# More of the gates' products behind the first scores of the sliding attention, fewer between its later units

## The reference, cut to what matters

```python
proj = u @ w_in            # xr, gr, q, k, v, g_rnn, g_attn
y_rnn  = rglru_branch(xr, gr, ...)          # recurrence, times gelu(gr)
y_attn = swa_sink_branch(q, k, v, sinks, cos, sin)
merged = sigmoid(g_rnn) * (y_rnn @ w_br_rnn) + sigmoid(g_attn) * (y_attn @ w_br_attn)
return merged @ w_out
```

## Time and profile before

| | |
|---|---|
| median of three runs | 2773.03 us (2770.18 to 2775.43) |
| the profiled execution | 2768.93 us, its span 2767.1 us |
| TensorE busy | 2613.5 us, 94% of the span |
| VectorE, ScalarE, GpSimd busy | 1281.7, 1090.0, 834.0 us |
| mean granted TensorE clock | 0.971 of full speed |
| sliding attention, layer 0 | 842.40 to 957.01 us of the span |
| sliding attention, layer 1 | 1834.22 to 1950.73 us |

### The profile page before, as it was taken

How to read it: one execution, slowest core, us unless ns; L and a number is a source line. 1 busy time by engine, 2 the same in 40 slices (tenths; PEclk the granted TensorE clock), 3 DMA queues, 4 the chain that set the end, 5 groups by cost and what they waited for, 6 DMA issues and landing times.

```text
span 2767.1 us, 30648 instructions
## 1 busy us (share of the span) xinstructions
PE 2613.5 (94%) x12190; PEld 2084.0 (75%) x12190; DVE 1281.7 (46%) x1841; ACT 1090.0 (39%) x1696; POOL 834.0 (30%) x354
## 2 busy tenths in 40 slices
PE   7889999999988999998999999989999999999997
PEld 5567877777765688877878888756788878788886
DVE  1775636767557646644351011466358353610113
ACT  2235224656445637323232122337365233332222
POOL 3220010000031244433234344322344432344444
PEclk9888999999999999999999999999999999999999
DMA  5141236889721133333123333221233331224232
GB/s 189 49 130 46 81 120 232 322 336 354 257 73 46 48 98 98 94 103 109 54 84 93 113 99 99 70 60 47 81 95 99 110 104 62 76 92 122 91 92 76
DMA packets 220077, 318.56 MB, mean 115 GB/s; under 512 B 17184, under 2 KB 176032, under 8 KB 219808
## 3 DMA queue, kind: packets, MB, share of 16 engines
q1 hardware_dynamic: 201184, 284.00, 32.2%
q10 hardware_dynamic: 16592, 24.72, 2.6%
q0 software_dynamic: 2160, 7.89, 0.8%
HBM read 300.81 MB, written 15.75 MB: 114 GB/s over the span
## 4 chain that ended last, share of the span: by engine, by line
PE 85%; DVE 8%; PEld 2%; ACT 2%; issue 2%; DMA 1%; ACTq 0%; PEldq 0%; DVEq 0%; POOL 0%
PE ps L624 79%; PE ps L771 3%; PE ps L636 3%; PEld ps L624 2%; DVE stats L1994 1%; DVE rows L2004 1%; DVE pair_l L2262 1%; DMA rows<-in_x 1%; DVE x_lo L1922 1%; DVE xc L2123 0%; DVE shift L2023 0%; ACT w_hi L1383 0%; ACT pair_h L1599 0%; DVE rows L2016 0%; DVE qf L2353 0%
## 5 line engine op out<-in xcount | busy, mean ns | idle before, releaser
L588 POOL TENSOR_TENSOR w_lo<-w_raw,w_hi 128x1024 fp32r<-128x1024 f32 x331 | 811.9, 2464 | 1554.7 <-ACT w_hi L1383 1554.7
L624 PE MATMUL ps<-x_hi,w_hi 128*128 128x512 f32 (+1 forms) x1624 | 656.1, 404 | 24.5 <-DVE x_lo L1922 16.3
L624 PE MATMUL ps<-x_lo,w_hi 128*128 128x512 f32 (+1 forms) x1624 | 642.1, 395 | 0.0
L624 PE MATMUL ps<-x_hi,w_lo 128*128 128x512 f32 (+1 forms) x1624 | 638.4, 393 | 0.0
L1383 ACT ACTIVATE w_hi<-w_raw 128x1024 fp32r<-128x1024 f32 x331 | 340.3, 1052 | 451.2 <-PE ps L624 447.8
L624 PEld LDWEIGHTS ps<-x_hi,w_hi 128*128 128x128 f32 (+1 forms) x1624 | 308.3, 190 | 110.6 <-POOL w_lo L588 21.7
L624 PEld LDWEIGHTS ps<-x_lo,w_hi 128*128 128x128 f32 (+1 forms) x1624 | 307.8, 190 | 70.4
L624 PEld LDWEIGHTS ps<-x_hi,w_lo 128*128 128x128 f32 (+1 forms) x1624 | 308.5, 190 | 68.8 <-issue 2.7
L2497 DVE TENSOR_TENSOR fhd<-fsg,ps 128x512 f32<-128x512 f32 x44 | 30.2, 687 | 391.8 <-PE ps L624 391.7
L2262 DVE TENSOR_TENSOR pair_l<-pair_raw,pair_h 128x2048 fp32r<-128x2048 f32 x84 | 189.8, 2287 | 47.1 <-ACT pair_h L1599 47.0
L1599 ACT ACTIVATE pair_h<-pair_raw 128x2048 fp32r<-128x2048 f32 x84 | 157.7, 1909 | 3.0 <-ACT yb L1614 2.8
(11 more groups left out here) (404 smaller groups left out, 4299.9 us busy)
## 6 DMA issues: line engine op xcount, KB each, us to landing
w_raw<-in_w_in SPq DMA_DIRECT2D x100, 512.0 KB, 3.7
w_raw<-in_ffn_wi SPq DMA_DIRECT2D x88, 512.0 KB, 3.5
pair_raw<-in_w_gate SPq DMA_DIRECT2D x56, 512.0 KB, 5.7
pair_raw<-in_w_up SPq DMA_DIRECT2D x56, 512.0 KB, 7.0
pair_raw<-in_w_down SPq DMA_DIRECT2D x56, 512.0 KB, 6.5
w_raw<-in_ffn_wo SPq DMA_DIRECT2D x44, 512.0 KB, 3.6
w_raw<-in_w_out SPq DMA_DIRECT2D x24, 512.0 KB, 3.6
kv_raw<-in_ckv_w SPq DMA_DIRECT2D x20, 512.0 KB, 4.5
```

What stands on the lines that cost most here:

```text
L588: pool.tensor_tensor(w_lo[:, slot, :], w_raw[:, slot, :], w_hi[:, slot, :].bitcast(F32), ALU.subtract).then_inc(lo_done, 1)
L624: ins = pe.matmul(o, a, b, start=first, stop=last)
```

## The change

TensorE's steps of the gates' products are dealt out differently: 8 behind the scores of unit 0, 2 behind unit 1, 1 behind unit 2, then 2 in each unit u, but only 1 where u % 7 is 2 or 5. The sum stays 64. Between the units that is 53 steps instead of 62, so nine are moved ahead. ScalarE's copies of the products and its splits of the slabs get written positions in place of the two conditions. Both layers have it. No instruction is added, removed or changed in size.

```diff
+    FILL_FIRST = (8, 2, 1)
+
+    def fill_steps(u):
+        return 1 if u % 7 in (2, 5) else 2
+
+    GATE_AT = (3, 7, 11, 16, 20, 25, 30, 34)
+    SPLIT_AT = (3, 5, 12, 15, 22, 25, 31, 33)
...
                 beside = gates_beside()
-                window_scores(0)
-                next(beside)
-                window_scores(1)
-                next(beside)
-                window_scores(2)
+                for u, steps in enumerate(FILL_FIRST):
+                    window_scores(u)
+                    for _ in range(steps):
+                        next(beside)
...
                     if u < last:
-                        next(beside)
-                        next(beside)
+                        for _ in range(fill_steps(u)):
+                            next(beside)
...
-                    if x >= 5 and x % 4 == 1:
-
-                        n = (x - 5) // 4
+                    if x in GATE_AT:
+                        n = GATE_AT.index(x)
                         product(n)
                         act.activation(mg[:, n, :], ps[:, 2 + n % 2, :], ACT.Copy).then_inc(s["evacuated"], 1)
-                    if x % 8 == 7 or (x % 8 == 1 and x > 1):
+                    if x in SPLIT_AT:
                         split(1)
```

More of the change, by code:

```diff
@@ L357, in build @@
     UNITS3 = [(i, p) for i in range(NT) for p in range(X_HEADS // 2)]
+    FILL_FIRST = (8, 2, 1)
+    def fill_steps(u):
+        return 1 if u % 7 in (2, 5) else 2
+    assert sum(FILL_FIRST) + sum(fill_steps(u) for u in range(len(UNITS2) - 1)) == KD * KD
+    GATE_AT = (3, 7, 11, 16, 20, 25, 30, 34)
+    SPLIT_AT = (3, 5, 12, 15, 22, 25, 31, 33)
     def width1(unit):
```

## The result

The changed kernel takes 2753.25 us (median of five runs, 2751.06 to 2759.23), the one before 2770.18 (five runs, 2769.36 to 2775.43). The ratio is 0.9936, 95% interval 0.9921 to 0.9951: 0.64% faster, 16.9 us between the medians. The profiled executions took 2768.93 and 2751.06 us, with spans of 2767.1 and 2749.3 us, 17.8 us apart. The forecast was a gain of 15.1 us.

What follows compares the result with a forecast made beforehand. TensorE was taken as the bound, with 6.4 us idle per layer before unit 1's scores, then half clock. 2 x (0.8 + 5.8) + 1.9 = 15.1 us off 2773.0 gave 2757.9 us; own range 2754 to 2763, 8-in-10 range 2753 to 2767.

Steps and rivals of the forecast that it cites:

- Part A: More steps behind the first scores: TensorE idles 1.8 us instead of 6.4, unit 3's scores 0.8 us sooner per layer.
- R4: Rival: steps behind the first scores wait for the second slab; margin 1.2 us, no time of its own, no chance given.
- Part B: Nine steps fewer between the units: 6.2 us minus 0.4 for VectorE lateness and GpSimd meetings, 5.8 us per layer.
- Part C: Layer 1's longer slow clock after the first scores: its extra 1.9 us goes if the clock doesn't fall.
- Part D: ScalarE's written positions for copies and splits: worth 0, at worst 1.6 us per layer.
- the best sum: Upper bounds over both layers: 2 x (0.9 + 6.2) + 1.9 = 16.1 us gain.
- 15.9 us without stalls: Gain over both layers if nothing stalled, set against 38 us of possible loss from GpSimd's subtractions.
- R1: Rival: the clock still falls after the first scores' remaining idle time; 6.5 us lost, 2764.4 us; chance 0.12.
- the row with 0.69: Evidence for a falling clock: idle 1.5 us at 1383.8, then mean clock 0.69 over the next 3.7 us.
- R2: Rival: ScalarE's and VectorE's latency sets the units' pace; only 3.5 us won, 2769.5 us; chance 0.09.
- R3: Rival: GpSimd's 16 subtractions hold up VectorE and so TensorE; at worst 38 us lost, 2795 us; chance 0.07.

Runs made afterwards that it cites:

- subtractions apart: Kernel before, its two splits at the tenth query evacuation moved to x = 1 and 3 of the units' loop; stages 111.81 and 113.05 us, whole 2763.91 us.
- single steps early: Changed kernel with its nine one-step units side by side at units 0 to 8, copies and splits matched; stages 110.41 and 110.40 us, whole 2757.45 us.
- clock alone: Kernel before plus 21 throwaway matmuls behind unit 0's scores, no work moved; stages 113.83 and 113.81 us, whole 2769.22 us.
- single steps late: Changed kernel with eight one-step units at units 23 to 30, copies and splits matched; stages 107.61 and 107.58 us, whole 2755.13 us.
- ten steps first: Changed kernel with ten steps behind the first scores, one-step units 0 to 2 and 23 to 30; stages 107.34 us, whole 2753.47 us, ratio 0.9931.

## Why the prediction came out as it did

**What bounds it: right.** The hole before unit 1's scores, VectorE as its cause and GpSimd behind that were read from the earlier trace rows; the run with the subtractions apart shows 3.8 of the 6.4 us to be GpSimd's hold.

**Part A, 0.8 us per layer: right.** The scores of unit 3 come 11.87 us after those of unit 0 instead of 12.63, 0.76 us sooner, with 11 steps done. The idle time is 1.71 us where 1.8 was worked out. The second slab was there in time, so R4 fell.

**Part B, 5.8 us per layer: too small.** From the scores of unit 3 on, 101.98 us became 95.74 in layer 0, 6.24, which is the full 9 x 0.69 us. The 0.4 us that I took off for VectorE being late at unit 9 and for meetings with GpSimd did not occur in either layer, though the meetings did: a division held for 2.54 us cost TensorE nothing. This is the term of the sum that was mis-sized: 5.8 where 6.24 was measured, 0.8 us over both layers. The single steps early show that the fear had its place (2.8 us), but not with the steps spread as they are.

**Part C, 1.9 us: right.** The layers are equal now; the run with the clock alone gives 2.70 - 0.78 = 1.92 us for it. The 1.9 us were taken from the one profile of before that the result is also measured against; whether another execution has the same difference is not shown.

**Part D, nothing: right as a sum, and too light as a warning.** All eight split places fit: TensorE waits for no slab. The old ones would have cost 9.8 and 9.1 us, more than the whole gain. The prediction named no price for a slab that comes late between the units, neither the wait (4.6 us) nor the half clock behind it (4.1 us).

**The sum and its range.** 15.1 was forecast for the two stages and 15.92 measured. The median is 4.7 us below the forecast of 2757.9. 0.8 of these are part B's. 2.85 are the base: with two more runs of the kernel before its median fell from 2773.03 to 2770.18 us. The last 1.0 is the rest of the difference of the medians, outside the stages (16.93 - 15.92). So the second step that failed is the range's lower end: 2754 allowed the best sum, 16.1 us, and 3 us for the spread of a median. The gain reached 15.92 of the 16.1, and base and rest together took 3.9 us where 3 were allowed. The runs of one kernel reach over 12 us (2746.6 to 2759.11), mostly from the part ahead of layer 0. The 15.9 us without stalls, which I had worked out, would have been the better middle. That the miss of the edge is only 0.75 us is luck: the median of the kernel before moved by 2.85 us with two more runs.

**The rivals.** R1 fell: with dense work ahead 1.7 us of idle time left the clock at 1.00 in all six profiles that had it. But the row with 0.69 in the earlier trace rows was a true warning, since 2.57 us did drop it. The row that I set against it, 1240 to 1244.2, ends where that idle time ends. The stretch behind it bears the reading out:

```profile
1244.20:1246.70 2.50, 1.74 (x12) 1.27 (x12) 2.09 (x8) 1.64 (x3) 0.00 (x0) 1.00 0.60 197
```

Both places of the earlier trace rows have the same instructions and the same idle times on TensorE (1.54 and then 0.71 us), and both have dense matmuls ahead of the transposes. The clock fell behind one and not behind the other, so the length of the idle time alone did not decide it. What did is open.

R2 fell, by the single steps late. R3 fell for the change, as no subtraction cost TensorE anything. In part that is timing which nobody planned. R3 feared the turns of queries 5 and 6 beside the two early subtractions; in both layers the subtractions met divisions instead. With less cover the mechanism does reach TensorE, as ten steps first and the single steps early show. The rule of the Trainium skill, page SBUF — State Buffer, section SBUF: two separate sides (GpSimd and a VectorE operation with two SBUF inputs or in a two-port mode lock each other out for a whole instruction), agrees with the held divisions and copies (2.54 and 1.75 us). By that page of the Trainium skill the one that starts first keeps the pair; the trace's records have the division of 859.53 first by 0.05 us, and yet it was the one held.

## What to carry to other kernels

Work that depends on nothing belongs in the one long hole of the busiest engine first, and only the rest between the units; a hole costs its length and then the half clock behind it, here up to 2.7 us for a hole of 6.4. Such a move drags the whole supply with it: count, for each moved step, when its slab must be split and when its bank must be empty, for a supply left at its old places cost more than the move gave. Where the changed stretches are 8% of the kernel, compare their own length between two events in the trace, and give the whole time a range as wide as its runs spread.

## What the runs showed of the hardware

TensorE's clock fell after idle time of 2.57 us (0.62 of full speed over the next 4.6 us in layer 0, 0.50 in layer 1), and did not after 1.7 us that followed eight dense steps. The two differ in the length of the idle time and in the work ahead of it, and no run changes one alone. The same idle time with the same schedule cost 1.2 us more in one layer than in the other.

VectorE's division L2408, which has one SBUF input and a column of scalars, is held by GpSimd as the copies are: 2.54 us instead of 0.35, though its record begins 0.05 us before the record of GpSimd's operation. A division whose record began 0.23 us ahead (918.38 against 918.61) took its usual 0.35 us. The maximum L2398, which also reads SBUF, was not held: it ran wholly beside the subtraction at 866.39 in 0.69 us, and so did the reciprocal behind it in 0.16. Six of the seven subtractions among layer 0's units met a division or a sink's copy and held it; the last, at 946.26, met nothing on VectorE.
